# Two transformer blocks on one core: start-up, first pair of heads, output projection and last layer rewritten

## The chip, the core and the metric

The kernel runs on one NeuronCore of a Trainium2 chip. The core has five engines with queues of their own: PE (matrix multiply), DVE (vector), ACT (scalar functions), POOL (GpSimd) and SP, which here only issues DMAs. They meet through semaphores alone. The metric is the device time of one launch in microseconds. The kernel before takes 2269.78 us, the median of three runs (2269.03 to 2270.07).

## The reference, cut to what matters

Everything is float32, for 512 tokens of width 1024. The first block computes

```python
mod = silu(c) @ w_ada + b_ada                      # 6 parts of 1024: sh1, sc1, g1, sh2, sc2, g2
h = layer_norm(x) * (1 + sc1) + sh1
q_a, k_a, v_a, f_a, q_c, k_c, v_c, gate_a, gate_c = split(h @ w_in)
o_a = forgetting_attention(q_a, k_a, v_a, f_a + b_f)      # 8 heads, log-decay F = cumsum(log_sigmoid)
o_c = chunk_band_attention(q_c, k_c, v_c, rel_bias)       # 8 heads
merged = sigmoid(gate_a) * (o_a @ w_br_fox) + sigmoid(gate_c) * (o_c @ w_br_chunk)
x = layer_norm(alpha * x + (1 + g1) * (merged @ w_out), ln1_g, ln1_b)
x = layer_norm(alpha * x + (1 + g2) * conv_ffn(...), ln2_g, ln2_b)
```

The second block puts 16 meta tokens ahead of the 512 (528 positions) and runs two layers on them: a latent attention with a convolutional feed-forward net, then a causal pooling mixer with another:

```python
h = concatenate([meta, x]);  L = 528
for i in range(2):
    h = h + rmsnorm(mixer_i(rmsnorm(h)))
    u = rmsnorm(h) @ w_up[i]                        # 1024 -> 5632
    u = conv_b + sum(conv_w[j] * u shifted by 2 - j)  # causal, width 3, along the positions
    f = (silu(gate) * val) @ w_down[i]              # 2816 -> 1024
    h = h + rmsnorm(f)
return h[:, 16:528]
```

Only positions 16 to 527 are returned. In the last layer nothing mixes positions but the convolution, which looks back by two.

## The kernel before

**Layout.** Activations lie transposed: 128 features on the partitions, positions along the free dimension, 8 tiles (KD = 8) for the width of 1024. Every product of float32 operands is made of three matmuls on rounded halves (`mm3`, L564): weights `w_hi` and `w_lo` against activations `H_hi` and `H_lo` (or `mid_hi`, `mg_hi` and so on). Weights stream from memory in blocks of 512 KB (`w_raw`, a ring of four slots). ACT rounds a block to `w_hi` (L1287), POOL subtracts to get `w_lo` (L1112), and PE uses it; a slot is filled again when POOL has lowered it, and rounded again when PE has used it.

**PSUM and halves.** For 512 positions a product has one span of 512 columns. For 528 positions it has two spans of 264 (`HALVES`, with `COL2` = 248 so that the cut falls on a bank's border), so each weight tile is loaded and streamed twice. The last four blocks of each closing projection are done half by half (`tail`), so that the norm of the first half runs beside the matmuls of the second.

**Stages.** They are, in order: `forget` (1 block), `qk` (4 turns of 4 blocks), `v` (2 turns of 4), an attention over 8 pairs of heads, `merge` (2 turns of 12), `out` (2 turns of 4), `up_a`, `down_a`, then for 528 positions `dqkv`, `uq`, `uk`, `uv`, an attention, `wo`, `up_b`, `down_b`, `pool`, `up_c` (11 turns of 4 blocks), `down_c` (2 turns of 12).

**The start.** SP issues, in this order: the vectors and constants, `X` in one DMA, the 16 meta columns into `X` in another, 4 blocks of `w_ada` (48 in all, 512 KB each, a ring `ada_w` of four slots), 4 weight blocks, 8 `ada`, 4 weights, 8 `ada`, then a loop of `ada` pairs with a weight block each. PE waits for `X` and meta, sums the tiles (L613), and after DVE has centred them (`XC`, L1816) and ACT squared them sums the squares (L625). The modulation: DVE multiplies each `ada` block by its column of `cond` and adds it into `ada_acc` (L1872, L1876; 8 blocks are one of the six parts), and PE sums `ada_acc` over the partitions (`ada_turn`, L812). Each 128x128 weight of it has one column moving; 8 matmuls show as 16 rows. Parts 1 and 0 (scale and shift) come ahead of `forget`, one more after each turn of `qk`. Then `H` is made tile by tile (DVE L1905, ACT L1429 and L1287, DVE L1848).

**The scan.** After `forget` DVE computes the decay F by a scan of nine doublings on 8 partitions (L1919 to L1939), and only then goes on to the `ada` part and the PSUM copies of the first turn of `qk`. F is first used by the attention.

**The first pair.** POOL's program is: lower all blocks up to the first four of `merge`, then for each pair `k_lo` (L1138) and `q_lo` (L1133, four times). The attention's first scores need `k_lo` and the first `q_lo`. ACT waits for the fourth merge block before the attention's first exponential.

**The output projection.** `pe.wait_ge(ml_ok, 12)` stands ahead of `out`: all eight tiles of `mg_hi`/`mg_lo` have to be there (DVE L2085, L2089, ACT L1287, DVE L2093) before the first matmul.

Of the kernel before, what the change touches and what calls it, by code (L numbers as in the profile page):

```python
# [54 lines left out]
for _name, _b, _t in STAGES:  # L55
# [9 lines left out]
    "forget": [(1, 0, 0)], "qk": [(4, 3, 0)], "v": [(4, 3, 0)],  # L65
# [52 lines left out]
COL2 = 248  # L118
HALF2 = S2 // 2
HALVES = ((0, HALF2), (HALF2, S2))  # L120

# [17 lines left out]
ADA_ORDER = (1, 0, 2, 3, 4, 5)  # L139


def program(nc, xT, meta, stream, ada, vecs, consts, rel, rope, yT):
    with ExitStack() as ctx:
# [9 lines left out]
        def sem(name):  # L153
# [32 lines left out]
            ("shift", SHIFT, F32), ("QK", 16 * S1, F32), ("XC", KD * S2, F32), ("ada_w", 4 * D, F32),  # L186
# [31 lines left out]
        x_in, cst_in, set_up, tab_in = sem("x_in"), sem("cst_in"), sem("set_up"), sem("tab_in")  # L218
        dve, act = sem("dve_step"), sem("act_step")

        ada_in = [sem(f"ada_in{i}") for i in range(4)]
        ada_used, ada_mm, cond_ok = sem("ada_used"), sem("ada_mm"), sem("cond_ok")
# [52 lines left out]
        def hf(t, k, s):  # L275
            return t[:, k * S2 + HALVES[s][0]:k * S2 + HALVES[s][1]]

        def psum_half(k, s):
            return PS[:, k, COL2 + HALVES[s][0]:COL2 + HALVES[s][1]]

# [207 lines left out]
        def _(sp):  # L488
            sp.dma_start(vec[:, :], vecs).then_inc(cst_in, 16)
            sp.dma_start(ident[:, :], consts[:, 0:P]).then_inc(cst_in, 16)  # L490
            sp.dma_start(work[:, 0:2 * P], consts[:, P:]).then_inc(cst_in, 16)
            sp.dma_start(X[:, :].rearrange("p (k t) -> p k t", k=KD)[:, :, META:S2],
                         xT.rearrange("k p t -> p k t")).then_inc(x_in, 16)
            sp.dma_start(X[:, :].rearrange("p (k t) -> p k t", k=KD)[:, :, 0:META],
                         meta.rearrange("k p t -> p k t")).then_inc(x_in, 16)
# [7 lines left out]
            def load_ada(n, slot):  # L503

                sp.wait_ge(ada_used, n + 1)
                sp.dma_start(ada_w[:, slot * D:(slot + 1) * D],
                             ada[ds(n, 1)].rearrange("a p c -> p (a c)")).then_inc(ada_in[slot], 16)

            for n in range(4):
                load_ada(n, n)  # L510
            for n in range(4):
                load_w(n, n)
            for n in range(4, 12):
                load_ada(n, n % 4)
            for n in range(4, 8):
                load_w(n, n % 4)
            for n in range(12, 20):
                load_ada(n, n % 4)
            with sp.Fori(0, 3) as g:
                for j in range(4):  # L520
                    for i in (2 * j, 2 * j + 1):
                        load_ada(g * 8 + (20 + i), i % 4)
                    load_w(g * 4 + (8 + j), j)
            for j in range(4):
                load_ada(44 + j, j)
                load_w(20 + j, j)
# [23 lines left out]
        def _(pe):  # L550
# [5 lines left out]
            def spans(T):  # L556
                return [(0, S1, 0)] if T == S1 else [(0, HALF2, COL2), (HALF2, S2, COL2)]

# [13 lines left out]
            def batch(name, bi, g, n, blocks, tiles, kks, cols, x, T, h_ready=None, between=None):  # L572

                done = 0
                for bi_, b in enumerate(blocks):
# [4 lines left out]
                    for m in range(tiles):  # L580
                        if bi_ == 0:
                            begin(name, bi, m, g)
                        for k in range(kk):
                            kt = done + k
                            if m == 0 and h_ready is not None:
# [3 lines left out]
                            last = mm3(PS[:, m, :], wtile(w_hi, slot, k, m, cols), wtile(w_lo, slot, k, m, cols),  # L589
                                       xh, xl, spans(T), bi_ == 0 and k == 0,  # L590
# [8 lines left out]
            def norm(n, T, ready, mean, src, four=0, bank=0, square_of=None):  # L599


                if mean:

                    first = 3 if four else 0
                    for k in range(first, n):
                        if four and k == first:
                            pe.wait_ge(x4_ok, four)
                        elif ready is not None:
# [195 lines left out]
            pe.wait_ge(set_up, SET_UP)  # L804
            pe.wait_ge(x_in, 32)
            norm(KD, S1, None, True, x1)

            def ada_turn(c):

                pe.wait_ge(ada_used, c * KD + (KD + 4))  # L810
                for m in range(KD):
                    last = pe.matmul(PS[:, 3, 512 + m:513 + m], ada_acc[:, m * P:(m + 1) * P], ones[:, 0:1],  # L812
                                     start=True, stop=True, skip_group_check=True)
                last.then_inc(ada_mm, 1)
# [26 lines left out]
            pe.wait_ge(free[0], FREE0["merge"][0] + 1)  # L841
            pe.wait_ge(f_ok, 1)
# [14 lines left out]
            pe.wait_ge(ml_ok, 12)  # L857
            with pe.Fori(0, 2) as g:
                batch("out", 0, g, g * 4 + BLK0["out"], range(4), 4, 2, 4,
                      lambda k: (mg_hi[:, k * S1:(k + 1) * S1], mg_lo[:, k * S1:(k + 1) * S1]), S1)  # L860
# [14 lines left out]
            def half_block(n, s, rows, k0, x, start, stop, begin_tile=None, told=0, teller=None, h_wait=None):  # L875

                slot = n % RING
                w_ready(n)
                for m in range(4):
                    if begin_tile is not None:  # L880
                        begin_tile(m)
                    for k in range(rows):
                        if m == 0 and h_wait is not None:
# [3 lines left out]
                                   [(*HALVES[s], COL2)], start and k == 0, stop and k == rows - 1)  # L887
# [8 lines left out]
            def sum_squares(name, s):  # L896
# [3 lines left out]
                if n == 4:  # L900
                    pe.wait_ge(sum4_ok, (1, 2, None, 3)[j])
                    pe.matmul(psum_half(0, s), ones[:, :], RS[:, HALVES[s][0]:HALVES[s][1]], start=True, stop=False)
                for m in range(n):
                    pe.wait_ge(sqm_ok[s], TAIL0[name] + m + 1)
                    last = pe.matmul(psum_half(0, s), ones[:, :], hf(work if n == 4 else sqx, m, s),
# [10 lines left out]
            def tail(name, x, rows):  # L916
# [4 lines left out]
                if nb > 4:  # L921
                    done = 0
                    for b in range(nb - 4):
                        slot = (n0 + b) % RING
                        w_ready(n0 + b)
                        for m in range(4):
                            if b == 0:
                                begin(name, 0, m, 1)
                            for k in range(rows[b]):
                                xh, xl = x(done + k)  # L930
                                last = mm3(PS[:, m, :], wtile(w_hi, slot, k, m), wtile(w_lo, slot, k, m), xh, xl,
                                           spans(S2), b == 0 and k == 0, False)
                        last.then_inc(w_used, 1)
                        done += rows[b]
                for s in range(2):
                    done = r0
                    for b in range(nb - 4, nb):
                        first, final = b == 0, b == nb - 1
                        last = half_block(n0 + b, s, rows[b], done, x, first, final,
# [8 lines left out]
            def head(name, before, s, h_base):  # L948

                for b in range(4):  # L950
# [8 lines left out]
                    last = half_block(BLK0[name] + b, s, 2, 2 * b, hx(S2), b == 0, b == 3,  # L959
# [145 lines left out]
        def _(gp):  # L1105
# [21 lines left out]
            def lower_heads1():  # L1127
# [17 lines left out]

                for p in range(PAIRS1):
                    lower_k(p)
# [1343 lines left out]
```

## Time and profile before

| what | value |
|---|---|
| median of three runs | 2269.78 us |
| the profiled execution's own time | 2268.35 us |
| its span in the trace | 2266.6 us |
| PE busy | 2031.6 us (90%), 12788 matmul rows |
| DVE, ACT, POOL busy | 948.3, 982.1, 867.0 us |
| mean granted TensorE clock | 0.956 of full |
| read from memory | 183.13 MB |

A matmul's row starts when it starts streaming; its end is modelled, so the time of one in a run is read from start to start or from a whole run of them, not from the mean duration. The idle time in brackets stands ahead of a row, with what ended it. The chain of waits follows the end of the program back to its start; what is not on it costs nothing.

### The profile page before, as it was taken

What the parts mean: (1) busy time and instruction counts of PE and PEld (TensorE: products, weight loads), DVE (VectorE), ACT (ScalarE), POOL (GpSimd) and SP (SyncE); (2) the same over time, 40 slices, a digit from 0 to 9 for tenths busy, and PEclk for the clock granted to TensorE, in tenths of its full rate; (3) what the DMA queues carried; (4) which work ended last, traced back from release to release, by engine and by line L of the source; (5) the groups of instructions that cost most, each with busy time, mean ns of one, the idle gap of its engine ahead of it and who ended that gap; (6) DMA issues with size and microseconds to landing.
All of it is one profiled execution on the core that took longest, in us unless ns stands there. A gap on an engine that the chain in (4) does not pass through costs nothing.

```text
span 2266.6 us, 35010 instructions
## 1 busy us (share of the span) xinstructions
PE 2031.6 (90%) x12788; PEld 1790.5 (79%) x12792; DVE 948.3 (42%) x1641; ACT 982.1 (43%) x1630; POOL 867.0 (38%) x506
## 2 busy tenths in 40 slices
PE   3699789998899999969888889999999569999997
PEld 2588667875577778849877789999999459999997
DVE  5862782125424241154577535324200773424102
ACT  2312573323545452244466445545522435545322
POOL 1244232432143434403533144443443644343443
PEclk8899999999999999989999899999999779999999
DMA  8372002222032323302200022232322003232332
GB/s 308 112 250 93 6 15 85 93 83 74 28 102 83 102 84 111 102 29 84 84 0 0 1 66 75 75 100 83 96 91 84 28 28 94 82 101 84 102 94 75
DMA packets 55404, 186.30 MB, mean 82 GB/s; under 512 B 6944, under 2 KB 10272, under 8 KB 55328
## 3 DMA queue, kind: packets, MB, share of 16 engines
q1 hardware_dynamic: 53920, 183.66, 25.6%
q10 hardware_dynamic: 1408, 1.59, 0.2%
q8 instruction: 52, 0.85, 0.1%
q14 instruction: 24, 0.20, 0.0%
HBM read 183.13 MB, written 2.10 MB: 82 GB/s over the span
## 4 chain that ended last, share of the span: by engine, by line
PE 79%; DVE 13%; ACT 3%; issue 3%; DMA 1%; POOL 1%; ACTq 0%; DVEq 0%; SPq 0%; POOLq 0%
PE PS L564 66%; PE PS L835 2%; PE PS L780 2%; PE PS L625 2%; PE PS L736 1%; PE PS L692 1%; PE PS L613 1%; DVE small L2022 1%; DVE ada_acc L1876 1%; DVE pool_s L298 1%; PE PS L753 1%; POOL X L1209 1%; DMA ada_w<-ada 1%; DVE work L2135 1%; PE PS L1064 1%
## 5 line engine op out<-in xcount | busy, mean ns | idle before, releaser
L1112 POOL TENSOR_TENSOR w_lo<-w_raw,w_hi 128x1024 fp32r<-128x1024 f32 x281 | 680.1, 2427 | 1080.8 <-ACT w_hi L1287 1080.7
L564 PE MATMUL PS<-H_hi,w_lo 128*128 128x264 f32 (+1 forms) x2152 | 584.1, 323 | 68.2 <-POOL H_lo L1249 26.4
L1287 ACT ACTIVATE w_hi<-w_raw 128x1024 fp32r<-128x1024 f32 (+2 forms) x317 | 309.5, 987 | 772.5 <-PE PS L564 708.8
L564 PE MATMUL PS<-H_lo,w_hi 128*128 128x264 f32 (+1 forms) x2152 | 575.2, 319 | 0.0
L564 PE MATMUL PS<-H_hi,w_hi 128*128 128x264 f32 (+1 forms) x2152 | 575.0, 319 | 0.0
L564 PEld LDWEIGHTS PS<-H_hi,w_lo 128*128 128x128 f32 x2152 | 365.0, 192 | 114.9 <-issue 45.8
L564 PEld LDWEIGHTS PS<-H_lo,w_hi 128*128 128x128 f32 x2152 | 367.0, 192 | 27.1
L564 PEld LDWEIGHTS PS<-H_hi,w_hi 128*128 128x128 f32 x2152 | 365.2, 191 | 28.0
L2135 DVE SCALAR_TENSOR_TENSOR work<-PS,vec,work 128x526 f32<-128x526 f32 (+3 forms) x264 | 188.3, 755 | 464.8 <-ACT work L1586 455.0
L564 PE MATMUL PS<-mid_hi,w_lo 128*128 128x264 f32 (+1 forms) x880 | 223.8, 308 | 3.6 <-DVE work L2135 3.6
L564 PE MATMUL PS<-mid_hi,w_hi 128*128 128x264 f32 (+1 forms) x880 | 223.1, 307 | 0.0
L564 PE MATMUL PS<-mid_lo,w_hi 128*128 128x264 f32 (+1 forms) x880 | 223.0, 307 | 0.0
L564 PEld LDWEIGHTS PS<-mid_hi,w_lo 128*128 128x128 f32 x880 | 146.4, 188 | 13.5 <-DVE work L2135 4.9
L564 PEld LDWEIGHTS PS<-mid_lo,w_hi 128*128 128x128 f32 x880 | 146.6, 188 | 7.8
L564 PEld LDWEIGHTS PS<-mid_hi,w_hi 128*128 128x128 f32 x880 | 146.4, 188 | 7.8
L1586 ACT ACTIVATE work<-PS,vec 128x528 f32<-128x528 f32 (+1 forms) x132 | 103.5, 788 | 75.2 <-PE PS L564 75.2
L1209 POOL TENSOR_TENSOR X<-X,work 128x264 f32<-128x264 f32 x64 | 54.0, 859 | 98.1 <-DVE work L2195 98.1
L1287 ACT ACTIVATE PT_hi<-PS 128x128 fp32r<-128x128 f32 (+4 forms) x144 | 58.3, 405 | 40.4 <-PE PS L692 27.1
L1876 DVE SCALAR_TENSOR_TENSOR ada_acc<-ada_w,cond,ada_acc 128x1024 f32<-128x1024 f32 x42 | 63.4, 1510 | 22.1 <-DMA ada_w<-ada 20.2
L2179 DVE TENSOR_SCALAR work<-PS 128x264 f32<-128x264 f32 x14 | 6.0, 430 | 155.1 <-ACT work L1400 155.1
L1532 ACT ACTIVATE work<-PS,small 128x128 f32<-128x128 f32 (+4 forms) x80 | 44.9, 561 | 52.2 <-DVE small L2022 51.9
L2103 DVE TENSOR_SCALAR work<-PS,modp 128x512 f32<-128x512 f32 x16 | 11.9, 745 | 132.1 <-PE PS L564 132.1
(268 smaller groups left out, 2999.8 us busy)
## 6 DMA issues: line engine op xcount, KB each, us to landing
w_raw<-stream SPq DMA_DIRECT2D x293, 512.0 KB, 3.6
ada_w<-ada SPq DMA_DIRECT2D x48, 512.0 KB, 5.8
X<-xT SPq DMA_DIRECT2D x1, 2048.0 KB, 9.0
yT<-X SPq DMA_DIRECT2D x8, 132.0 KB, 1.7
rel_raw<-rel ACTq DMA_DIRECT2D x4, 256.0 KB, 2.7
yT<-X SPq DMA_DIRECT2D x8, 124.0 KB, 1.7
vec<-vecs SPq DMA_DIRECT2D x1, 390.0 KB, 2.8
sin_t<-rope ACTq DMA_DIRECT2D x1, 264.0 KB, 2.7
```

Source lines behind the costliest of these rows:

```text
L298: chain.done(e.tensor_tensor(padded(n, a, b), padded(at[k], a, b), padded(at[k], a - step, b - step), ALU.add))
L564: last = pe.matmul(out[:, c0 + a:c0 + b], w, x[:, a:b], start=start and i == 0, stop=stop and i == 2)
L625: last = pe.matmul(PS[:, bank, c0 + a:c0 + b], ones[:, :], square[:, a:b], start=k == 0, stop=k == n - 1)
L780: last = pe.matmul(PS[:, 3, 256 + a:256 + b], l[0:kn, vo:vo + P], r[0:kn, so + a:so + b], start=par == 0 and j == 0 and n_ == 0, stop=par ...
L835: last = pe.matmul(PS[:, t, 0:512], l[:, hs], r[:, wr], start=kt == 0 and j == 0, stop=kt == 7 and j == 2)
L1112: gp.tensor_tensor(w_lo[:, o], w_raw[:, o], w_hi[:, o].bitcast(F32), ALU.subtract)\
L1209: gp.tensor_tensor(hf(X, k, s), hf(X, k, s), hf(work, k % 2, s), ALU.add).then_inc(xh_ok[s], 1)
L1287: return act_.activation(out, in_, ACT.Copy, scale=scale)
L1532: act_.activation(ht(work, t % 2, S2)[0:qn, 0:ke], PS[0:qn, t % 2, c0:c0 + ke], ACT.Exp, bias=small[0:qn, t % 2:t % 2 + 1], accum_out=smal ...
L1586: act_.activation(ht(work, m, T), psumT(m, T), ACT.Identity, bias=v1("conv", g * 16 + (c + 3)), scale=v1("conv", g * 16 + (c + 2)))\
L1876: ins = v.scalar_tensor_tensor(ada_acc[:, :], w, cond[:, k:k + 1], ada_acc[:, :], ALU.mult, ALU.add)
L2135: ins = v.scalar_tensor_tensor(y[:, s:], u[:, :T - s], w, y[:, s:], ALU.mult, ALU.add)
```

## The change

It has four parts.

1. **The start.** `X` comes as eight DMAs with a semaphore each, and the first sum of PE takes each tile as it comes; the meta columns are loaded later, the vectors and constants from ACT's queue. The `ada_w` ring has eight slots. In the first two parts of the modulation DVE accumulates five blocks, and PE takes the other three (`ADA_PE` = 5, 6, 7) straight from `ada_w` against the column of `cond`, ahead of the sum over `ada_acc`. Between the squares' sum and `forget` PE now has 2 x 32 of these one-column matmuls in place of 2 x 8. `H` is made in place from `XC`: DVE weighs it by scale and deviation (four tiles of it ahead of the shift), ACT adds the shift and rounds, DVE subtracts. `forget` writes bank 3, so that `qk` starts on other banks. The scan goes behind the four turns of `qk`, `sel_bf` behind `forget`.
2. **The first pair.** POOL lowers `k` and the first `q` ahead of the first four merge blocks, the other three `q` behind them; ACT's wait for the fourth merge block stands at its second step.
3. **The output projection** waits for `ml_ok` tile by tile.
4. **The last layer.** `up_c` leaves out columns 0 to 13, `down_c` and its norm 0 to 15 (`FIRST`). The cut of 528 positions is at 272 rather than 264 for all layers, so spans are 272 and 256, in `up_c` 258 and 256, in `down_c` 256 and 256.

```diff
-COL2 = 248
-HALF2 = S2 // 2
+HALF2 = 272
+COL2 = 512 - HALF2
+FIRST = {"up_c": META - 2, "down_c": META}
+ADA_PE = (5, 6, 7)
+ADA_DVE = KD - len(ADA_PE)
...
 # SP
-            sp.dma_start(X[...][:, :, META:S2], xT...).then_inc(x_in, 16)
-            sp.dma_start(X[...][:, :, 0:META], meta...).then_inc(x_in, 16)
+            for k in range(KD):
+                sp.dma_start(X[:, k * S2 + META:(k + 1) * S2], xT[k]).then_inc(x_in[k], 16)
...
 # PE
+            def ada_rows(w, col, start, stop):
+                for m in range(KD):
+                    last = pe.matmul(PS[:, 3, 512 + m:513 + m], w[:, m * P:(m + 1) * P], col, start=start and m == 0,
+                                     stop=stop, skip_group_check=True)
+                return last
...
+                    for i, k in enumerate(ADA_PE):
+                        pe.wait_ge(ada_in[k], 16 * (c + 1))
+                        ada_rows(ada_w[:, k * D:(k + 1) * D], cond[:, k:k + 1], i == 0, False).then_inc(ada_pe, 1)
+                    pe.wait_ge(ada_used, (c + 1) * ADA_DVE)
...
-            pe.wait_ge(ml_ok, 12)
             with pe.Fori(0, 2) as g:
                 batch("out", 0, g, g * 4 + BLK0["out"], range(4), 4, 2, 4,
-                      lambda k: (mg_hi[...], mg_lo[...]), S1)
+                      lambda k: (mg_hi[...], mg_lo[...]), S1, (ml_ok, 4))
...
 # POOL
+                lower_k(0)
+                lower_q(0, 0)
+                lower_blocks(BLK0["merge"], BLK0["merge"] + RING)
                 for p in range(PAIRS1):
-                    lower_k(p)
-                    lower_q(p, 0)
+                    if p:
+                        lower_k(p)
+                        lower_q(p, 0)
...
-            lower_blocks(0, BLK0["merge"] + RING)
+            lower_blocks(0, BLK0["merge"])
             lower_heads1()
...
 # ACT
-                act_.wait_ge(w_lo_ok, BLK0["merge"] + 2 * RING)
                 for n in range(STEPS1):
+                    if n == 1:
+                        act_.wait_ge(w_lo_ok, BLK0["merge"] + 2 * RING)
...
+            act_.wait_ge(shift_ok, 2)
+            for k in range(KD):
+                act_.wait_ge(t_ok, k + 1)
+                act_.activation(ht(H_hi, k), ht(XC, k), ACT.Identity, bias=mod[:, k:k + 1]).then_inc(t_hi, 1)
...
 # DVE
+            def weigh_xc(k):
+                x = ht(XC, k)
+                v.scalar_tensor_tensor(x, x, modp[:, 8 + k:9 + k], RS[:, 0:S1], ALU.mult, ALU.mult).then_inc(t_ok, 1)
```

PE's queue from the start to the first matmuls of `forget`, before (`ada_acc` is the accumulated part, `ones` a column of ones):

```order
L613 MATMUL PS<-X,ones 128x512 x8
L625 MATMUL PS<-work,ones 128x512 x8
L812 MATMUL PS<-ones,ada_acc 128x1 x16
L564 MATMUL PS<-H_hi,w_lo 128x512
L564 MATMUL PS<-H_lo,w_hi 128x512
```

and now, at the same place:

```order
L641 MATMUL PS<-X,ones 128x512 x8
L653 MATMUL PS<-work,ones 128x512 x8
L837 MATMUL PS<-cond,ada_w 128x1 x24
L837 MATMUL PS<-ones,ada_acc 128x1 x8
L837 MATMUL PS<-cond,ada_w 128x1 x24
L837 MATMUL PS<-ones,ada_acc 128x1 x8
L590 MATMUL PS<-H_hi,w_lo 128x512
```

Sixteen one-column matmuls have become 64 between the squares' sum and `forget`.

POOL's queue at the end of `v` and the start of the attention, before (the first row is the fourth merge block, the rest the first two pairs of heads):

```order
L1112 TENSOR_TENSOR w_lo<-w_raw,w_hi 128x1024
L1138 TENSOR_TENSOR k_lo<-QK,k_hi 128x512
L1133 TENSOR_TENSOR q_lo<-QK,q_hi 128x128 x4
L1138 TENSOR_TENSOR k_lo<-QK,k_hi 128x512
L1133 TENSOR_TENSOR q_lo<-QK,q_hi 128x128 x4
```

and now (the first row is the last block of `v`):

```order
L1156 TENSOR_TENSOR w_lo<-w_raw,w_hi 128x1024
L1182 TENSOR_TENSOR k_lo<-QK,k_hi 128x512
L1177 TENSOR_TENSOR q_lo<-QK,q_hi 128x128
L1156 TENSOR_TENSOR w_lo<-w_raw,w_hi 128x1024 x4
L1177 TENSOR_TENSOR q_lo<-QK,q_hi 128x128 x3
L1182 TENSOR_TENSOR k_lo<-QK,k_hi 128x512
```

`k_lo` and one `q_lo` have moved ahead of four blocks; three `q_lo` still stand behind them.

## Rows read from the trace of the kernel before

**Rows 1.** The page, part 4: the chain that ended last, by engine.
```profile
PE 79%; DVE 13%; ACT 3%; issue 3%; DMA 1%; POOL 1%; ACTq 0%; DVEq 0%; SPq 0%; POOLq 0%
```

**Rows 2.** Timeline of the start: start us, length us, engine, line, operation, count, idle before.
```profile
12.85 8.88 PE L613 MATMUL PS<-X,ones 128*128 128x512 f32 x16 [12.85 <-DMA X<-meta]
21.84 4.87 DVE L1816 SCALAR_TENSOR_TENSOR XC<-PS,X 128x512 f32<-128x512 f32 x8 [2.50 <-PE PS L613]
24.61 7.13 PE L625 MATMUL PS<-work,ones 128*128 128x512 f32 x16 [2.88 <-ACT work L1339]
46.65 5.45 DVE L1876 SCALAR_TENSOR_TENSOR ada_acc<-ada_w,cond,ada_acc 128x1024 f32<-128x1024 f32 x4 [4.32 <-DMA ada_w<-ada]
52.15 3.57 PE L812 MATMUL PS<-ones,ada_acc 128*128 128x1 f32 x16 [15.72 <-DVE ada_acc L1876]
71.19 0.50 PE L564 MATMUL PS<-H_hi,w_lo 128*128 128x512 f32 x1 [0.83 <-DVE work L1914]
```

**Rows 3.** Windows: length, busy by engine, granted clock, DMA share, GB/s.
```profile
35.00:40.00 5.00, 1.43 (x13) 1.34 (x13) 4.63 (x9) 0.00 (x0) 0.00 (x0) 0.69 0.86 315
50.00:55.00 5.00, 2.85 (x14) 2.85 (x14) 1.99 (x2) 0.00 (x0) 0.00 (x0) 0.50 0.78 296
60.00:65.00 5.00, 4.77 (x12) 2.56 (x10) 4.55 (x7) 4.78 (x7) 0.00 (x0) 0.58 0.00 0
```

**Rows 4.** The qk turns and v: the first from the timeline, the rest the chain.
```profile
107.23 3.57 PE L812 MATMUL PS<-ones,ada_acc 128*128 128x1 f32 x16 [13.37 <-DVE ada_acc L1876]
...
110.81 24.62 PE PS L564 x96
135.42 1.68 PE PS L812 x16
137.10 22.50 PE PS L564 x96
...
185.46 44.82 PE PS L835 x192
```

**Rows 5.** Timeline of DVE: the scan's first and last row, the first V_lo.
```profile
73.21 0.68 DVE L1919 SCALAR_TENSOR_TENSOR work<-work 8x512 f32<-8x512 f32 x1 [1.36 <-ACT work L1619]
...
90.14 2.51 DVE L1939 CAST F_bf<-work 8x512 bf16<-8x512 f32 x1
...
204.60 0.69 DVE L1954 TENSOR_TENSOR V_lo<-PS,V_hi 128x512 f32 x1 [17.21 <-ACT V_hi L1287]
```

**Rows 6.** Timeline where v ends and the attention starts.
```profile
232.01 2.34 POOL L1112 TENSOR_TENSOR w_lo<-w_raw,w_hi 128x1024 fp32r<-128x1024 f32 x1 [3.77 <-ACT w_hi L1287]
...
235.53 1.70 POOL L1133 TENSOR_TENSOR q_lo<-QK,q_hi 128x128 fp32r<-128x128 f32 x4
...
236.13 0.58 PE L648 MATMUL PS<-k_hi,q_lo 64*128 64x256 f32 x2 [5.86 <-POOL q_lo L1133]
...
237.82 0.58 PE L648 MATMUL PS<-k_hi,q_lo 64*128 64x256 f32 x2
```

**Rows 7.** Timelines where merge ends and out starts, PE and DVE.
```profile
491.90 0.63 PE L564 MATMUL PS<-O_split,w_hi 128*128 128x512 f32 x2
497.76 0.79 PE L564 MATMUL PS<-mg_hi,w_lo 128*128 128x512 f32 x1 [5.23 <-DVE mg_lo L2093]
...
494.94 2.49 DVE L2093 TENSOR_TENSOR mg_lo<-acc,mg_hi 128x512 f32 x4
```

**Rows 8.** Chain in up_c and down_c, then PE's timeline in the attention.
```profile
1880.32 233.92 PE PS L564 x1908
2118.57 119.11 PE PS L564 x972
...
296.48 0.28 PE L692 MATMUL PS<-PT_lo,V_hi 128*128 128x256 f32 x1
297.44 0.22 PE L692 MATMUL PS<-PT_hi,V_lo 128*128 128x128 f32 x1
297.61 0.28 PE L692 MATMUL PS<-PT_hi,V_hi 128*128 128x128 f32 x1
```

## What the change is predicted to do

> **What bounds the kernel now.** I read the chain of waits first, then the timeline along it, then windows for the clock and the busy shares. The chain is PE's for 79% and DVE's for 13% [rows 1]: a matmul saved in a long stage counts in full, and what else can be won lies in the gaps between stages. Four stretches matter here.
>
> The start: PE's first matmul waits for the meta columns until 12.85. The sum over `X` takes 8.88, `XC` follows, and the squares' sum ends at 24.61 + 7.13 = 31.74. PE then has little to do until 52.15, because DVE waits for `ada` blocks (its four additions from 46.65 begin with such a wait). The first `qk` matmul comes at 71.19 [rows 2]. It is followed by a second hole: PE waits 13.37 for DVE's third `ada` part, and the turn's end is 110.81 [rows 4]. DVE was late because it did the scan first, from 73.21 to 90.14 + 2.51 = 92.65 [rows 5].
>
> The hand-over from `v` to the attention: `v` ends at 185.46 + 44.82 = 230.28 [rows 4], the first scores start at 236.13, after POOL has lowered a merge block (232.01 to 234.35), then `k` and `q` [rows 6].
>
> The entry to `out`: `merge` has its last matmul pair at 491.90, and `out` begins at 497.76 after an idle time of 5.23 [rows 7].
>
> `up_c` and `down_c`: unbroken PE pieces of 233.92 and 119.11 [rows 8].
>
> **Part 1, the start.** *First sum.* PE can begin with the first of eight tiles, some 4 us in; the meta columns no longer stand behind `X`. The lower bound of the sum's end is 4 + 8.88 = 12.9, the upper one that the last tile comes at 12.85 as now and 0.9 (two cold matmul rows at most) follows: 13.8. I take 13.5 against 21.73. *Squares.* `XC` from 13.6, PE's squares 1.5 later (one `XC`, one square; now it is 2.77, with ACT rounding weights in the way), so they end at 15.2 + 7.13 = 22.3, 9.4 earlier than now [rows 2].
>
> *Modulation.* A group of 8 one-column matmuls (16 rows) costs 1.68 at full clock [rows 4] and 3.57 at half [rows 2]. Each of the first two parts has four such groups now in place of one. The clock is what decides. After the squares' sum it fell in the window from 35, whose mean of 0.69 puts the fall near 36.9, some 5.2 after the last wide matmul. In the window from 50 it stays at 0.50 while the one-column group runs, and it rises only in the window from 60 (0.58, so near 64.2) [rows 3], after `H`'s matmuls have begun; likewise the turn that follows the group at 107.23 takes 24.62 where a warm one takes 22.50 [rows 4], so the group had not brought the clock up. I therefore take one-column matmuls as no work that holds the clock. From 22.3: two groups warm to 25.8, the third half and half to 28.0, the fourth cold to 31.6. DVE adds 0.4 and tells PE; the second part has four cold groups, 14.3, and ends at 46.3. DVE's five products (0.75 + 4 x 1.3 = 5.9; the 1.3 from the four in 5.45) are hidden by it. Their blocks are there: with eight slots the second part's loads go out from about 19 to 28, as DVE and PE let slots go. The SP queue holds in front of these loads one weight block without a wait.
>
> The Trainium skill ("TensorE: Matmul & The Clock Gate", Part 1, What's actually happening) says that activity of the array releases the throttle, with no word on how narrow a matmul may be. Read plainly it would keep all eight groups warm; rows 3 and 4 say otherwise so far.
>
> *Forget.* Shift at 46.5, ACT 0.8, DVE 0.7: the first `H` tile at 48.1. The tiles come every 1.4 (two DVE passes of 0.69 [rows 5]) for four, then every 0.7 to 0.8; PE, at first cold, needs up to 1.3 a tile at twice 22.50 / 96 = 0.234 a matmul. That is 8 to 10.3; `qk` starts at 57 (bounds 56 and 58.5) against 71.19. No pass of the old form is missing on the path: ACT does one pass a tile in place of two.
>
> *qk.* The scan is gone from DVE's queue here. DVE has 1.4 of work on `forget` and 1.7 for `sel_bf`, then 9.9 for the third part, done at 70; its PSUM copies are due at 57 + 18. So the wait of 13.37 goes. Every later turn already costs 22.50 + 1.68 with the same `ada` and weight loads, four slots even; in SP's queue a pair of `ada` loads stands behind a weight load that waits for POOL, as before, and the slack is a turn. The first turn ends at 57 + 22.5 + 1.7 = 81.2. Now it ends at 110.81, with 2.12 more lost on a cold clock behind it [rows 4]. Gain: 112.9 - 81.2 = **31.7**.
>
> *The scan behind it.* It starts 1.9 into `v` and takes 19.4, up to 21.3. The first `V_lo` comes now at 204.60, 19.14 into `v` [rows 5]; it will come 2.2 later. Bank 0 is free at 22.1 and PE wants it at 44.82 / 2 = 22.4. The cover is thin: 0 to 1 us, I take 0.
>
> **Part 2, the first pair.** `k_lo` and the first `q_lo` are done long before `v` ends, so scores 0 start at 230.3. Scores 1 need the second `q_lo`, which stands in POOL's queue behind the fourth merge block: 234.35 + 0.43 (a quarter of 1.70) = 234.8, against 237.82 [rows 6]. From there on nothing changes. ACT's moved wait is over at 234.35 too, before its second step. Gain **3.0**, not the whole 5.86; bounds 2.5 and 5.
>
> **Part 3, `out`.** The first two blocks use only the first four tiles, which `merge`'s first turn left long ago, and last 2 x 5.6 = 11.2 us; the tiles of the second turn are there at 494.94 + 2.49 = 497.4, five us after `out` could begin. The banks come free before 494.94, one ahead of each 1.4 us of matmuls. So PE goes from 492.4 (491.90 and two matmuls) straight on: 5.4 [rows 7]. Also the clock, which falls in the present hole, stays up: 2.12 by rows 4 for a cold restart; here the hole is shorter, I take 1.6. Gain **7.0**, bounds 5.0 and 7.5.
>
> **Part 4, the last layer.** `up_c` has 44 x 8 x 3 = 1056 pairs of matmuls and `down_c` 8 x 22 x 3 = 528. They lose 14 and 16 columns a pair. A 264-wide matmul takes 233.92 / 1920 = 0.1218 (40 x 4 x 2 x 3 x 2 of them; the chain's 1908 lacks a few), a 512-wide one 0.2344 [rows 8, 4]: 0.454 ns a column. The pairs would save 6.4 and 7.3 ns: 6.7 + 3.8 = 10.5. The timeline has eight 256-wide ones in 297.44 - 296.48, so 0.12 each [rows 8]; two would be 0.240 against 0.2437, and the saving only 3.9 + 2.0 = 5.9. I take **9.5**, nearer to the slope from the two long pieces. The new cut elsewhere moves 8 columns from one span to the other and leaves the sum; at most half a us either way around the norms.
>
> **Sum.** 31.7 + 3.0 + 7.0 + 9.5 = 51.2. The profiled execution took 2268.35 (its span 2266.6 and 1.75 around it), so 2217.2; the median of the runs stands 1.4 above it: **2218.6**.
>
> **Rivals.**
>
> *Warm one-column groups (0.2).* If 64 of them in a row do hold the clock up, eight groups cost 1.7 each. The first part ends at 29.2; DVE's 5.9 then bounds the second (35.5), its last group ends at 37.2, and `qk` starts near 48: 9 less, 2209.5. For it: PE is busier there than it ever was with such work. Against it: rows 3. This is the result that the skill's rule, quoted above, would give.
>
> *The head starves on loads (0.25).* 48 `ada` blocks, 24 weight blocks and `X` (40 MB) are now to come in some 140 us in place of 170. The windows have 296 to 315 GB/s when the queue is busy [rows 3]; a turn wants 6.3 MB in 24.2, 260 GB/s. If weights and `ada` get in each other's way by 3 to 4 us a turn, or `X` and the first eight blocks share the engines so that the first sum ends at 17, the gain shrinks by 10: 2229. Against it: the present turns from 137 on run at 22.50 and 1.68 with those loads.
>
> *Slower than before (0.01).* The 128-wide matmuls from 297.44 to 297.61 take 0.085 each, 0.66 ns a column against 0.46 [rows 8]. If that dearer rate began at 258 columns, with the start at column 14 that no present span has, `up_c`'s 2112 matmuls would cost 0.171 in place of 0.119: +110, 2329. It outweighs the gain from 24 ns a matmul on. Against it: eight 256-wide ones at 0.12.
>
> *A part does nothing (0.04):* some further wait stands where the `out` or the start hole was, and 2240 or so results.
>
> **How the numbers follow.** The forecast has 0.5, its own range 2213 to 2224 (start +-3, part 4 +-3, the others 1 to 2). Warm 0.2, starved 0.25, the last two 0.05. The range that holds 8 in 10 is 2205 to 2232. A measurement tells 0.2%, about 4.5 us, from no change; every case but the last lies beyond it on the fast side: faster 0.98, same 0.01, slower 0.01.
>
> **What would show it.** Right, step by step: PE's first matmul before 5; the squares' sum ending near 22; groups of 3.57 in the second part; `qk` from 55 to 59, no idle time of PE until `v` ends; scores 1 near 4.5 after `v`; no idle time before `out` and a clock of 1.0 there; pairs of 0.237 to 0.240 in `up_c`. Wrong: groups of 1.7 throughout, DVE waiting for `ada` DMAs inside a `qk` turn, PE waiting for `V_lo` in the middle of `v`, or `up_c` at 0.2437 a pair.

## The result, and the profile of the changed kernel

| | before | changed |
|---|---|---|
| median (lowest to highest), us | 2269.41 (2268.08 to 2270.07), 4 runs | 2216.32 (2215.77 to 2219.24), 4 runs |
| profiled execution, its span, us | 2268.35, 2266.6 | 2215.77, 2213.8 |

The ratio is 0.9769 (95% interval 0.9752 to 0.9786): 53.1 us less, where 51.2 were forecast.

The page after, part 4, the chain by engine. To [rows 1]: PE has 3 points more of it and DVE 2 fewer.

```profile
PE 82%; DVE 11%; ACT 3%; issue 2%; POOL 1%; ACTq 0%; DMA 0%; DVEq 0%; POOLq 0%
```

The start, from timelines of PE, DVE and ACT, in the order of [rows 2] (start us, length us, engine, line, operation, count, idle before):

```profile
4.29 8.59 PE L641 MATMUL PS<-X,ones 128*128 128x512 f32 x16 [4.29 <-DMA X<-xT]
13.03 4.88 DVE L1881 SCALAR_TENSOR_TENSOR XC<-PS,X 128x512 f32<-128x512 f32 x8 [5.27 <-PE PS L641]
14.43 7.13 PE L653 MATMUL PS<-work,ones 128*128 128x512 f32 x16 [1.55 <-ACT work L1388]
21.40 7.55 PE L837 MATMUL PS<-cond,ada_w 128*128 128x1 f32 x48
28.81 3.55 PE L837 MATMUL PS<-ones,ada_acc 128*128 128x1 f32 x16
32.69 10.40 PE L837 MATMUL PS<-cond,ada_w 128*128 128x1 f32 x48 [0.33 <-DVE mod L1954]
33.62 7.36 DVE L1942 SCALAR_TENSOR_TENSOR ada_acc<-ada_w,cond,ada_acc 128x1024 f32<-128x1024 f32 x4
42.95 3.55 PE L837 MATMUL PS<-ones,ada_acc 128*128 128x1 f32 x16
48.40 0.76 PE L590 MATMUL PS<-H_hi,w_lo 128*128 128x512 f32 x1 [1.89 <-DVE H_lo L1993]
```

PE starts at 4.29 on the first tile of `X`, where it waited for the meta columns until 12.85. The squares end at 21.56 instead of 31.74, and from there PE has one-column matmuls almost without a gap until 46.5, where it had mostly stood idle. DVE's four additions begin long before PE is through: they no longer end anything.

Windows of the changed kernel (length, busy by engine, granted clock, DMA share, GB/s), to [rows 3]:

```profile
20.00:25.00 5.00, 5.00 (x35) 4.16 (x33) 4.71 (x5) 2.27 (x3) 1.02 (x1) 0.94 1.03 404
25.00:30.00 5.00, 5.00 (x25) 5.00 (x25) 3.28 (x3) 1.06 (x1) 1.40 (x2) 0.50 1.00 369
40.00:45.00 5.00, 5.00 (x25) 5.00 (x25) 3.63 (x5) 0.00 (x0) 0.00 (x0) 0.50 1.02 406
50.00:55.00 5.00, 4.95 (x19) 3.41 (x18) 4.88 (x8) 2.82 (x4) 1.65 (x1) 0.83 0.07 29
455.00:460.00 5.00, 5.00 (x23) 4.03 (x22) 4.90 (x9) 2.93 (x5) 0.00 (x0) 1.00 0.34 105
```

PE is busy for 5.00 of 5.00 and yet at half clock, with one-column matmuls alone. The clock fell about 24.4 (0.94 over the first window) and rose in the window from 50, after `forget` had begun at 48.40. In the last window, where `out` begins, it is 1.00. The DMA engines are full in the three windows up to 45, at 369 to 406 GB/s.

The chain of waits (start us, length us, what; to [rows 4] and [rows 8]):

```profile
52.28 26.15 PE PS L590 x111
78.43 1.68 PE PS L837 x16
80.11 22.50 PE PS L590 x96
...
152.65 44.81 PE PS L878 x192
...
1349.03 235.01 PE PS L590 x1908
1588.36 118.89 PE PS L590 x972
...
1837.16 228.97 PE PS L590 x1908
2070.38 115.12 PE PS L590 x972
```

The wait of 13.37 in the first `qk` turn is gone: the turn ends at 80.11 instead of 110.81, and the next one takes 22.50 instead of 24.62. `v` starts at 152.65 instead of 185.46.

DVE and PE round `v` and the first scores, to [rows 5] and [rows 6]:

```profile
169.25 0.42 DVE L2037 CAST F_bf<-work 8x512 bf16<-8x512 f32 x1
171.79 0.69 DVE L2043 TENSOR_TENSOR V_lo<-PS,V_hi 128x512 f32 x1 [2.12 <-ACT V_hi L1336]
197.38 0.39 PE L676 MATMUL PS<-k_hi,q_lo 64*128 64x256 f32 x2
202.09 0.58 PE L676 MATMUL PS<-k_hi,q_lo 64*128 64x256 f32 x2 [3.66 <-POOL q_lo L1177]
```

The scan ends at 169.67, 17.0 into `v`, DVE is then idle for 2.12, and the first `V_lo` comes 19.14 into `v`, as before. Scores 0 start as `v` ends; the wait has moved to scores 1 and is 3.66.

How the gain grows, from the rows above and those of before:

| reached | before | changed | gain so far |
|---|---|---|---|
| squares' sum ends | 31.74 | 21.56 | 10.2 |
| first `qk` turn ends | 110.81 | 80.11 | 30.7 |
| `v` starts | 185.46 | 152.65 | 32.8 |
| scores 1 | 237.82 | 202.09 | 35.7 |
| `out` starts | 497.76 | 456.17 | 41.6 |
| `up_b` starts | 1392.11 | 1349.03 | 43.1 |
| the end | 2266.6 | 2213.8 | 52.8 |

### The profile page after: what moved, and what is told of

It is laid out like the page before. It is cut to its first block, busy times and chain, and to the rows that moved or that the text cites. A ratio compares the mean times of both kernels' runs of the same rounds, so it can differ in the third digit from the quotient of the medians.

```text
span 2213.8 us, 35187 instructions
## 1 busy us (share of the span) xinstructions
PE 2033.6 (92%) x12884; PEld 1797.2 (81%) x12888; DVE 949.4 (43%) x1635; ACT 973.7 (44%) x1622; POOL 869.4 (39%) x506
## 4 chain that ended last, share of the span: by engine, by line
PE 82%; DVE 11%; ACT 3%; issue 2%; POOL 1%; ACTq 0%; DMA 0%; DVEq 0%; POOLq 0%
PE PS L590 68%; PE PS L878 2%; PE PS L653 2%; PE PS L808 2%; PE PS L837 1%; PE PS L764 1%; PE PS L720 1%; PE PS L641 1%; DVE small L2111 1%; POOL X L1258 1%; DVE pool_s L315 1%; PE PS L781 1%; DVE work L2226 1%; DVE work L2287 1%; PE PS L1108 1%
## 5 line engine op out<-in xcount | busy, mean ns | idle before, releaser
L590 PE MATMUL PS<-H_hi,w_lo 128*128 128x272 f32 (+3 forms) x2152 | 580.1, 321 | 61.9 <-POOL H_lo L1298 25.9
L590 PE MATMUL PS<-H_lo,w_hi 128*128 128x272 f32 (+3 forms) x2152 | 573.5, 318 | 0.0
L590 PE MATMUL PS<-H_hi,w_hi 128*128 128x272 f32 (+3 forms) x2152 | 573.0, 318 | 0.0
L2226 DVE SCALAR_TENSOR_TENSOR work<-PS,vec,work 128x512 f32<-128x512 f32 (+4 forms) x264 | 187.0, 751 | 462.1 <-ACT work L1641 452.3
L590 PE MATMUL PS<-mid_hi,w_lo 128*128 128x256 f32 (+2 forms) x880 | 222.6, 306 | 3.6 <-DVE work L2226 3.5
L590 PE MATMUL PS<-mid_hi,w_hi 128*128 128x256 f32 (+2 forms) x880 | 221.5, 305 | 0.0
L590 PE MATMUL PS<-mid_lo,w_hi 128*128 128x256 f32 (+2 forms) x880 | 221.2, 304 | 0.0
L1641 ACT ACTIVATE work<-PS,vec 128x512 f32<-128x512 f32 (+1 forms) x132 | 102.7, 783 | 75.2 <-PE PS L590 75.2
L1258 POOL TENSOR_TENSOR X<-X,work 128x256 f32<-128x256 f32 (+1 forms) x64 | 53.7, 854 | 97.7 <-DVE work L2287 97.7
L1336 ACT ACTIVATE PT_hi<-PS 128x128 fp32r<-128x128 f32 (+4 forms) x144 | 58.3, 405 | 43.2 <-PE PS L720 27.0
L2271 DVE TENSOR_SCALAR work<-PS 128x256 f32<-128x256 f32 (+1 forms) x14 | 6.0, 429 | 152.7 <-ACT work L1450 152.7
```

Of the source, the lines that this page charges most:

```text
L590: last = pe.matmul(out[:, c0 + a:c0 + b], w, x[:, a:b], start=start and i == 0, stop=stop and i == 2)
L1258: gp.tensor_tensor(x, x, hf(work, k % 2, s, name), ALU.add).then_inc(xh_ok[s], 1)
L1336: return act_.activation(out, in_, ACT.Copy, scale=scale)
L1641: act_.activation(ht(work, m, T)[:, a:], psumT(m, T)[:, a:], ACT.Identity, bias=v1("conv", g * 16 + (c + 3)), scale=v1("conv", g * 16 + (c ...
L2226: ins = v.scalar_tensor_tensor(y[:, b:], u[:, b - s:T - s], w, y[:, b:], ALU.mult, ALU.add)
```

## Experiments

Each is the changed kernel with one edit. Each ran 4 times beside the kernel before. The three groups ran apart, on different chips; the kernel before had medians of 2270.49 (part 4 and `out`), 2271.13 (first pair, two blocks, one wide matmul in four, scan) and 2270.17 (the rest). The changed kernel was run again in the third only, so a total of another group is compared with it across chips, and up to 1.0 of such a difference means nothing.

**The changed kernel once more**, for a comparison on the same chip.

> The changed kernel itself, beside the three others of this call on the same chip. Both theories: 2216 to 2219.

Measured 2218.35 (2217.34 to 2219.09), ratio 0.9773 (0.9756 to 0.9789). Its `v` starts at 154.19, 1.5 later than in the first profile. The first sum took 9.81 instead of 8.59 as the tiles of `X` came later, and PE waited once for an `ada` block (the last row):

```profile
4.28 9.81 PE L641 MATMUL PS<-X,ones 128*128 128x512 f32 x16 [4.28 <-DMA X<-xT]
34.10 10.37 PE L837 MATMUL PS<-cond,ada_w 128*128 128x1 f32 x48 [1.66 <-DMA ada_w<-ada]
```

The runs that leave the head alone are further samples of it: in the seven profiles with this head `v` starts at 152.65 to 155.42, and the first profile is the earliest. It is also the only one of the seven without a wait for an `ada` block ahead of the second part; the others waited 1.1 to 2.8. So the head varies by up to 3 us between executions, and totals that differ by less show little. Where I could, I compared stages.

**Part 4 undone: every span and both cuts as before.**

```
-HALF2 = 272
+HALF2 = 264
-FIRST = {"up_c": META - 2, "down_c": META}
+FIRST = {"up_c": 0, "down_c": 0}
```

> The changed kernel with the fourth part taken back: nothing is skipped in the last layer, the cut is at 264 again. Theory (columns): up_c and down_c get back what they lost. The prediction's 9.5 us on 2216.3 give 2225.8; the traces of before and after put it at 4.95 us in the ten long turns of up_c (0.5 more in the first), 4.0 in down_c and 0.6 behind, so 2226. Rival (the saving of 9 to 10 us in the last layer came partly from elsewhere, a clock or an earlier load): under 2222.

**The skipped columns undone, the cut at 272 kept.**

```
-FIRST = {"up_c": META - 2, "down_c": META}
+FIRST = {"up_c": 0, "down_c": 0}
```

> The changed kernel with nothing skipped in the last layer, but with the new cut (spans of 272 and 256 in all layers). Theory (a matmul's time is proportional to its columns): the same time as a1_no_part4 within 0.5 us. Rival (a 256-wide matmul is dearer than its share of columns): up_b's ten long turns went from 233.92 to 235.01 us with the same sum of columns, so up_b and up_c cost 1.1 us each more than in a1_no_part4, 2 us in all; part of it may come back around the norms, where the second half is shorter.

**The skipped columns kept, the cut at 264** (halves of 250 and 264 columns in `up_c`, 248 and 264 in `down_c`).

```
-HALF2 = 272
+HALF2 = 264
```

> The changed kernel with the same columns skipped, but the old cut at 264: spans of 250 and 264 in up_c, 248 and 264 in down_c. Theory (proportional): the same as the changed kernel, 2216 within 1.5 us. Rival (the slower-than-before rival of the prediction, a dearer rate for narrow matmuls, with its edge at 256): 250 columns at the 0.66 ns a column of the 128-wide ones are 0.165 us in place of 0.114, 1056 + 528 times: +80 us, 2296.

The chains of the three in `up_b`, `down_b`, `up_c` and `down_c`:

```profile
1354.99 233.88 PE PS L590 x1908
1593.21 119.11 PE PS L590 x972
1843.16 233.91 PE PS L590 x1908
2081.41 119.11 PE PS L590 x972
```
```profile
1353.19 235.02 PE PS L590 x1908
...
1841.78 235.04 PE PS L590 x1908
2081.13 118.90 PE PS L590 x972
```
```profile
1351.94 233.93 PE PS L590 x1908
...
1839.84 229.38 PE PS L590 x1908
2073.48 114.81 PE PS L590 x972
```

| | median | ratio (95%) | from `up_b`'s start to the end |
|---|---|---|---|
| part 4 undone | 2227.59 | 0.9807 (0.9791 to 0.9823) | 874.4 |
| cut at 272 only | 2227.48 | 0.9808 (0.9792 to 0.9825) | 875.3 |
| skipped, cut at 264 | 2219.02 | 0.9774 (0.9758 to 0.9790) | 865.2 |
| changed kernel again | 2218.35 | 0.9773 (0.9756 to 0.9789) | 864.9 |

The last column is the span less the chain's first start; it was 874.5 before. Part 4 is worth 9.5 by it and 9.2 by the medians. All of it comes from the skipped columns; the cut alone makes `up_b` and `up_c` 1.1 dearer each, of which 0.9 remains in the last column and nothing can be seen in the medians. With the cut at 272 the skipping is worth 10.4 (875.3 less 864.9), with the cut at 264 it is worth 9.2 (874.4 less 865.2). Halves of 250 and 248 columns show no dearer rate: `up_c` takes 229.38, and the rival that put a step there, at 2296, is out. So is the prediction's rival of a dearer rate from 258 columns and a start at column 14: the changed kernel has just these and takes 228.97.

**`out` waits for all twelve again.**

```
+            pe.wait_ge(ml_ok, 12)
...
-                      ..., S1, (ml_ok, 4))
+                      ..., S1)
```

> The changed kernel with one wait for all twelve counts ahead of the output projection again. Theory: the idle time of 5.2 us and a cold restart come back, 2216.3 + 7.0 = 2223.3 (the traces say 7.1 between the end of merge and the end of out). Rival (the time would have been lost behind anyway, at the banks): under 2219.

Measured 2225.09 (2223.1 to 2227.0), ratio 0.9797 (0.9780 to 0.9813): 6.7 above the changed kernel's second run. Its head was 1.1 later by chance (`v` at 155.29), but from `merge`'s start to `out`'s end it takes 184.9 against 176.9 there and 175.3 in the first profile. The waits by line (total, times, longest) and the window have the hole and the clock back:

```profile
PE PS L590 <- DVE mg_lo L2183: 5.2, 1, 5.2
```
```profile
460.00:470.00 10.00, 4.77 (x15) 3.53 (x14) 6.59 (x11) 4.75 (x6) 2.85 (x1) 0.79 0.14 52
```

**POOL lowers the first pair behind the `merge` blocks, as before.**

```
-                lower_k(0)
-                lower_q(0, 0)
-                lower_blocks(BLK0["merge"], BLK0["merge"] + RING)
...
-            lower_blocks(0, BLK0["merge"])
+            lower_blocks(0, BLK0["merge"] + RING)
```

(with ACT's wait put back ahead of its first step too)

> The changed kernel with POOL's and ACT's order at the start of the first attention as before (k and q of the first pair behind the four merge blocks). Theory: 2216.3 + 3.3 = 2219.6, by the traces (scores 1 come 2.9 us earlier after the end of v, the attention's end 3.3). Rival (the first exponentials and the transposes catch up on their own): 2217.

Measured 2220.14 (2219.71 to 2220.72), ratio 0.9780 (0.9763 to 0.9796): 1.8 above the changed kernel's second run, too near its spread. The rows are clear:

```profile
204.04 0.58 PE L676 MATMUL PS<-k_hi,q_lo 64*128 64x256 f32 x2 [5.86 <-POOL q_lo L1177]
```

Scores 0 start 5.86 after `v` and scores 1 at 205.74, 7.54 after it, where the changed kernel has 4.63: the order is worth 2.9. From `v`'s start to `merge`'s it takes 172.0 against 169.1 and 168.7 in the two profiles of the changed kernel, so the 2.9 lasts through the attention, or a little more.

**PE takes two blocks of each part, DVE six.**

```
-ADA_PE = (5, 6, 7)
+ADA_PE = (6, 7)
```

> The changed kernel with PE taking two of the eight ada blocks of the first two parts (6 and 7), DVE six. Theory (PE is the bound there, as its one-column groups of 16 rows cost 3.57 us on the cold clock): a group less on PE in each part. The second part falls from 13.8 to 10.7 us, the first from 10.8 to about 8, until DVE (its six products, then the four steps of the deviation) is the bound: 5 us less in all, 2211. Rival (DVE is the bound): the same or slower, 2216 to 2218.

Measured 2218.18 (2216.14 to 2218.62), ratio 0.9768 (0.9752 to 0.9785): nothing lost, nothing won. In the first part DVE became the bound, by 2.44, since one of its five products took 3.19 in place of 1.30 while POOL lowered a block; in the second part PE waited for an `ada` transfer. PE's timeline:

```profile
28.87 3.57 PE L837 MATMUL PS<-ones,ada_acc 128*128 128x1 f32 x16 [2.44 <-DVE ada_acc L1942]
...
36.37 6.96 PE L837 MATMUL PS<-cond,ada_w 128*128 128x1 f32 x32 [3.93 <-DMA ada_w<-ada]
```

**Two blocks, and POOL's first lowering held back until DVE's products are done.**

```
-ADA_PE = (5, 6, 7)
+ADA_PE = (6, 7)
...
+            gp.wait_ge(ada_used, 2 * ADA_DVE)
```

> As b2_pe_two_blocks (PE takes two of eight ada blocks), and POOL lowers its first weight block only when DVE has done the products of the second part. Theory (in b2_pe_two_blocks a product of each part took 3.19 in place of 1.30 us beside a lowering of POOL, and DVE was the bound): DVE's chain is 1.9 shorter in each part, until the landing of PE's ada blocks is the bound in the second; 2 to 3.5 us less than the changed kernel beside it. Rival (the loads that wait for the lowered weight blocks come too late for the third part, or PE's blocks land no earlier): the same or slower than the changed kernel.

Measured 2217.31 (2217.12 to 2219.27), ratio 0.9771 (0.9755 to 0.9787), 1.0 under the changed kernel beside it, within its spread. DVE's five products of a part take 6.85, where they took 8.74 in the run above, but the time goes into a wait for the `ada` load and into DVE's four steps on `XC` beside POOL's postponed lowering:

```profile
35.56 6.96 PE L837 MATMUL PS<-cond,ada_w 128*128 128x1 f32 x32 [5.21 <-DMA ada_w<-ada]
...
38.38 9.03 DVE L1984 SCALAR_TENSOR_TENSOR XC<-XC,modp,RS 128x512 f32<-128x512 f32 x4
```

Those four took 2.73 in the changed kernel beside it. `v` starts at 153.53 against 154.19.

**A 512-column bf16 matmul into an unused bank ahead of every four one-column matmuls**, in the first two parts.

```
+                    if warm and m % 4 == 0:
+                        pe.matmul(PS[:, 2, 0:512], ident_bf[:, :], F_bf[:, 0:512], start=True, stop=True)
```

(PE also waits for `F_bf` and `ident_bf` to be set ahead of them; no idle time shows there)

> The changed kernel with a wide bf16 matmul of 512 columns, whose result is never read, put ahead of every four of the one-column matmuls of the first two parts (16 in all, 0.23 us each warm). Theory (one-column matmuls don't hold the clock up, wide ones do): the clock stays at 1.0 from 25 to 50 us, the groups cost 1.7 + 0.46 in place of 3.57, the second part is bound by DVE near 9 us, qk starts 5 to 8 us earlier: 2209 to 2211. Rival (two wide ones in a group are too little to count, or the clock fell for another reason): the groups cost 3.57 + 0.86 and the kernel takes 2222.

Measured 2224.47 (2222.24 to 2225.99), ratio 0.9796 (0.9779 to 0.9812): slower by 6.1 than the changed kernel's second run, and my theory of it was wrong. PE's timeline shows the fall at 26.86, where the wide one goes from 0.38 to 0.53 and eight rows of one-column matmuls from 0.95 to 1.71; the window from 40 stays at half:

```profile
25.83 0.38 PE L839 MATMUL PS<-F_bf,ident_bf 128*128 128x512 bf16 x1
26.05 0.95 PE L840 MATMUL PS<-cond,ada_w 128*128 128x1 f32 x8
26.86 0.53 PE L839 MATMUL PS<-F_bf,ident_bf 128*128 128x512 bf16 x1
27.18 1.71 PE L840 MATMUL PS<-cond,ada_w 128*128 128x1 f32 x8
```
```profile
40.00:45.00 5.00, 5.00 (x24) 4.82 (x25) 4.90 (x5) 0.00 (x0) 2.27 (x1) 0.50 1.07 381
```

**The same ahead of every one-column matmul.**

```
-                    if warm and m % 4 == 0:
+                    if warm:
```

> The changed kernel with a wide bf16 matmul of 512 columns, never read, ahead of every one of the 64 one-column matmuls of the first two parts. [...] A group costs 1.7 + 8 x 0.22 = 3.5 us, the same as now on the cold clock, and what follows starts warm, so the head ends where it does now, within 1.5 us, and the kernel takes 2216 to 2219. Rival (the clock falls whatever runs beside one-column matmuls): groups of 3.57 + 8 x 0.43 = 7.0 us, the second part alone 14 us longer, 2240 or more.

Measured 2219.13 (2216.48 to 2223.5), ratio 0.9782 (0.9764 to 0.9799). Now the clock is 1.00 in every window from 15 to 55, this one among them:

```profile
40.00:45.00 5.00, 4.92 (x43) 4.62 (x44) 4.87 (x5) 0.00 (x0) 1.13 (x1) 1.00 1.02 384
```

A wide and a one-column matmul come every 0.353, so a group is 2.8 instead of 3.57 although it holds twice the matmuls. `v` starts at 151.48, 2.7 earlier than in the changed kernel beside it; `merge` starts only 1.1 earlier, and the total is the same within the spread. Of the other 1.6, 0.5 is gone by 205, within the first scores, and 1.1 between 267 and 283, at one load of the attention. The chain has it, and DVE's timeline the wait:

```profile
271.46 4.04 DMA rel_raw<-rel
```
```profile
275.53 0.62 DVE L2055 TENSOR_SCALAR rel_raw<-rel_raw,vec 128x256 f32<-128x256 f32 x2 [1.86 <-DMA rel_raw<-rel]
```

The four such loads took 2.6 to 2.8 each in the changed kernel beside it. One of the four was slow in both kernels with two blocks too (3.95 and 4.54). Why, the runs do not tell.

**The scan ahead of the `qk` turns on DVE, as before.**

```
+            # the scan's 30 lines stand here
             def take_qk(g):
                 ada_part(2, g)
...
-            # and no longer here, behind loop(4, 2, take_qk)
```

> The changed kernel with the scan ahead of the four turns of qk on DVE again. Theory (the second hole of before came from the scan in DVE's queue): the scan takes 19.4 us from 59, DVE's third part is done near 89 in place of 70, PE's turn 0 is over at 76.7, so PE waits some 10 us and restarts cold with the group and the turn (1.9 + 2.1): 2216.3 + 14 = 2230. Rival (it came from the ada loads, which the eight slots have cured): within 3 us of 2216.

Measured 2233.03 (2231.2 to 2234.34), ratio 0.9834 (0.9817 to 0.9850). PE's wait is back:

```profile
PE PS L837 <- DVE ada_acc L1942: 10.2, 1, 10.2
```

`v` starts at 167.41, 13.2 later than in the changed kernel's second run, and the total is 14.7 higher, of which up to 1.0 can be the other chip. PE's wait is 10.2 here and was 13.37 in the kernel before, which had the scan at the same place but four `ada_w` slots: there DVE, once through with the scan, waited for `ada` blocks as well, 0.75 and 1.85.

**PE waits for all eight tiles of `X` before the first sum.**

```
+            for k in range(KD):
+                pe.wait_ge(x_in[k], 16)
```

> The changed kernel with PE waiting for all eight tiles of X ahead of its first sum. Theory (the sum's start at the first tile is worth what the last tile comes later, as all behind it is one chain): the last tile lands near 10 us, the sum ends near 19 in place of 13 to 14, +5.5 us. Rival (the ada blocks or DVE would be the bound a little later anyway): within 2 us of the changed kernel.

Measured 2223.14 (2222.38 to 2224.19), ratio 0.9793 (0.9777 to 0.9809): 4.8 slower.

```profile
10.85 9.42 PE L641 MATMUL PS<-X,ones 128*128 128x512 f32 x16 [10.85 <-DMA X<-xT]
```

The first sum ends at 20.27 against 14.09, and `XC` starts at 20.41 against 14.23. `v` starts at 161.03, 6.8 later; of this 1.0 comes back by the end of the span, and the medians differ by less still.

## Why the prediction was right

**Part 1, the start (31.7 forecast, 32.8 measured).** The sum begins on the first tile and ends at 12.88 (forecast 13.5, bounds 12.9 and 13.8); with all tiles first it ends 6.2 later, and the kernel takes 4.8 more. The squares end at 21.56 (22.3). The clock is the step that was most in doubt, and it went as [rows 3] said: groups of 3.4 to 3.6 in the second part, which ends at 46.50 (46.3). The first part was 1.7 dearer than I had it (10.96 against 9.3), since the clock fell 2.8 after the last wide matmul and not 5.2 after it (4.0 in the second profile). A slip is in my sum as well: a group half warm and half cold costs 2.6, not the 2.2 that I added. `forget` gave this back, with the clock up again at 51.7, so that `qk` began near 55.9 (57, bounds 56 and 58.5). So the sum of the head has errors of both signs, and that it agrees to 1.1 is in part luck. The rival of warm groups is refuted by the windows.

The Trainium skill ("TensorE: Matmul & The Clock Gate", Part 1, What's actually happening) lets activity of the engine release the throttle; read plainly the groups would have been warm, and this trace does not agree: 0.50 with PE busy for 5.00 of 5.00.

Two more terms of this part were wrong and cost little. DVE's third `ada` part took 16.05 and not 9.9, as its seven products ran for the most part beside POOL's lowering (in the run with the scan first, where POOL stood idle during them, seven took 9.21):

```profile
59.96 15.28 DVE L1942 SCALAR_TENSOR_TENSOR ada_acc<-ada_w,cond,ada_acc 128x1024 f32<-128x1024 f32 x7
```

It was through at 75.24 instead of 70, 3.0 before PE's next group of one-column matmuls began at 78.27. And the blocks were not all there: see the loads below. With the head of the six other profiles, where `v` starts at 153.38 to 155.42, the gain of part 1 is 30.0 to 32.1.

What the single steps of the start are worth was not all taken apart. From the kernel before to the changed one, `qk` begins 15.3 earlier, 10.2 of it at the squares' end. No run undoes the late meta columns, the eight slots, PE's share of the blocks as a whole, or the new form of `H`.

**The scan.** With it behind `qk`, and with the eight slots, the wait of 13.37 is gone from the first turn; the experiment that puts the scan alone back has a wait of 10.2 and costs 13 to 15 in all: the largest of the steps that were undone one by one. Of the 13.37 the prediction blamed on the scan, DVE's waits for `ada` blocks behind it were a part. That it costs nothing in `v` was the thin cover of the forecast, 0 to 1 us. It held, with 2.12 of DVE's idle time to spare, because the scan ended 17.0 into `v` and not 21.3: two of its instructions took over 2 us beside POOL's lowering (2.27 and 2.51), where four had in the kernel before (2.25 to 2.51).

**Part 2, the first pair (3.0 forecast, 2.9 by the experiment, 2.9 to 3.3 by the traces).** The wait did not go but moved to the second `q_lo` behind the fourth block: 3.66 of 5.86 remain.

**Part 3, `out` (7.0 forecast; 7.1 by the traces, 6.7 by the experiment).** From 35.7 at scores 1 and 36.1 where `merge` starts, the gain is 43.2 at `out`'s end: 5.5 at its start, the rest from the clock that stays up.

**Part 4, the last layer (9.5 forecast; 9.7 by the traces, 9.5 and 9.2 by the experiment).** The total was right, but by two terms that make up for each other. With the cut at 272 in both kernels, leaving the columns out takes `up_c` from 235.04 to 228.97, which is 6.3 ns for each of 960 pairs (6.4 by the slope), and 10.4 off the whole (10.5 by the slope). I took 9.5, between the slope and the eight 256-wide matmuls, without a row that said how far; that it came out is luck. The term that was mis-sized is the cut: I had the sum of columns unchanged and at most half a us around the norms, and by itself it costs 1.1 in `up_b`, 1.1 in `up_c` and 0.9 in all. Together with the skipping it brings nothing that can be told from noise (865.2 with the cut at 264, 864.9 with it at 272). From before to changed, `up_b` is 1.1 dearer, `up_c` 4.95 and `down_c` 4.0 cheaper; 0.9 comes back between `down_b` and `up_c`, of which the cut by itself brings 0.5. What the rest of it is, the runs do not tell.

**The loads.** The rival that had the head starved did not come about as a whole: no `qk` turn of the changed kernel waits for `ada`. It showed at its edge. I had written that the blocks of the second part are there; in the first profile they were, in the six others with this head PE waited 1.1 to 2.8 for one, and both kernels with two blocks a part ran into that load (3.93 and 5.21). From 30 to 50 the DMA engines moved 379 to 414 GB/s in the two profiles of the changed kernel, so a step of PE or DVE shortened there is likely to end in such a wait.

**What I had wrong in the experiments.** That two wide matmuls a group hold the clock up; that PE stays the bound with two blocks; that holding POOL back gives 2 us or more.

## What to carry to other kernels

When an engine comes late with its share of a stage, look first at what it does ahead of it: moving one 19 us job behind its neighbour was worth more than any other step that was undone by itself here. Price a moved or split step with the clock that it will have, read from a stretch of the same kind of work, since busy time alone did not tell it. And after a hole is closed, name the next thing in the queue (here a second `q_lo`, an `ada` load) before counting the whole wait as won.

## What the runs showed of the hardware

- One-column fp32 matmuls alone left TensorE at 0.50 while PE was busy without a gap. A 512-column bf16 one ahead of every four did not change that; one ahead of each kept it at 1.00, and 16 matmuls a group were then faster than 8 (2.8 against 3.57).
- No step shows in a matmul's time between 248 and 264 columns: with the columns left out, `up_c` and `down_c` together took 344.19 with a cut at 264 and 344.09 with one at 272. It is not quite in proportion to the columns either: nothing left out, `up_b` took 233.88 in spans of 264 and 264, and 235.02 in spans of 272 and 256.
- A DVE instruction that starts beside POOL's lowering can last until that lowering ends, even a small one: a copy of 8 x 2 elements took 2.25 and one of 8 x 64 took 2.28, against 0.14 to 0.17 for others of up to 8 x 32. A product took 3.19 against 1.30. Not every instruction beside a lowering is held up so. The first of the copies ended at 63.90, which is also when the first of POOL's two blocks did (61.03, and half of 5.73). With the scan ahead of `qk`, DVE's timeline has

```profile
61.65 2.25 DVE L2012 COPY work<-work 8x2 f32<-8x2 f32 x1
...
68.18 0.17 DVE L2012 COPY work<-work 8x16 f32<-8x16 f32 x1
```
